# One core, a two-block transformer kernel: U and V expert gathers interleaved by head, V rows summed half on TensorE and half on VectorE

## The reference

```python
act = jax.nn.gelu(jnp.einsum('tkd,td->tk', expert_u[ib], xb))
return jnp.einsum('tk,tkd->td', act * gb, expert_v[ib])
```

## Time and profile before

| | us |
|---|---|
| three runs, median (lowest to highest) | 2695.06 (2687.06 to 2697.92) |
| the profiled execution | 2693.59 |
| its span | 2692.2 |
| busy VectorE / TensorE matmul / GpSimd / ScalarE | 1981.9 / 1236.9 / 1051.8 / 545.4 |
| first gather of the ring | at 613.11 |
| first transposes of h behind the last V row | at 1864.95 |

### The profile page before, as it was taken

The page is one execution under the profiler, slowest core; times in us unless marked ns, Lnnn a source line. Parts: engine busy times, 40 slices in busy tenths (PEclk is TensorE's granted clock), DMA queues, the critical chain, the costliest instruction groups (busy, mean ns, idle before and its releaser), DMA issues.

```text
span 2692.2 us, 14997 instructions
## 1 busy us (share of the span) xinstructions
PE 1236.9 (46%) x5498; PEld 1015.7 (38%) x5498; DVE 1981.9 (74%) x1974; ACT 545.4 (20%) x587; POOL 1051.8 (39%) x522
## 2 busy tenths in 40 slices
PE   7988886520000000000000000002999999999999
PEld 6876665420000000000000000002778878788887
DVE  3456557778999999999999999998454474654453
ACT  4244342110000000000000000001443343543342
POOL 0000001327877676768888888884000000000000
PEclk9999888765555555555555555556999999999999
DMA  5432346668999898989999999997445544445554
GB/s 212 155 131 104 110 160 238 243 221 360 422 422 420 347 377 355 375 357 414 422 422 422 422 422 422 422 422 286 160 156 190 200 150 157 171 173 192 195 184 147
DMA packets 104473, 750.93 MB, mean 279 GB/s; under 512 B 11856, under 2 KB 11856, under 8 KB 13264
## 3 DMA queue, kind: packets, MB, share of 16 engines
q0 software_dynamic: 73728, 536.90, 49.0%
q1 hardware_dynamic: 28512, 207.63, 21.7%
q10 hardware_dynamic: 2160, 5.45, 0.5%
HBM read 747.84 MB, written 2.10 MB: 279 GB/s over the span
## 4 chain that ended last, share of the span: by engine, by line
PE 35%; DVE 23%; POOL 23%; DMA 9%; issue 6%; ACT 3%; ACTq 0%; DVEq 0%; SPq 0%; POOLq 0%
POOL W L236 12%; PE ps L268 11%; POOL xT_rows L236 11%; PE ps L270 11%; PE ps L269 11%; DVE h L1365 10%; DMA W<-in_expert_u,idx 5%; DVE wlo L986 3%; DMA xT_rows<-in_expert_u,idx 3%; DVE W L1287 2%; ACT whi L639 1%; PE ps L295 1%; DVE xT_rows L1337 1%; DMA W<-in_expert_v,idx 1%; DVE tmp L1274 0%
## 5 line engine op out<-in xcount | busy, mean ns | idle before, releaser
L986 DVE TENSOR_TENSOR wlo<-raw,whi 128x2048 fp32r<-128x2048 f32 x195 | 446.4, 2290 | 372.3 <-ACT whi L639 372.0
L295 PE MATMUL ps<-ident,h 128*128 128x128 f32 x128 | 19.7, 310 | 1299.7 <-DVEq L1370 1289.7
L268 PE MATMUL ps<-whi,xT 128*128 128x512 f32 (+1 forms) x1432 | 576.4, 403 | 86.5 <-DVE wlo L986 84.7
L269 PE MATMUL ps<-wlo,xT 128*128 128x512 f32 (+1 forms) x1432 | 568.4, 397 | 0.0
L270 PE MATMUL ps<-whi,xT 128*128 128x512 f32 (+1 forms) x1432 | 567.7, 396 | 0.0
L236 POOL DMA_INDIRECT W<-in_expert_u,idx x144 | 280.7, 1949 | 585.1 <-DVE idx L1280 421.6
L295 PEld LDWEIGHTS ps<-ident,h 128*128 128x128 f32 x128 | 17.8, 162 | 1301.7 <-DVEq L1370 1290.2
L639 ACT ACTIVATE whi<-raw 128x2048 fp32r<-128x2048 f32 x195 | 372.8, 1914 | 492.6 <-PE ps L270 474.3
L268 PEld LDWEIGHTS ps<-whi,xT 128*128 128x128 f32 x1432 | 279.5, 195 | 155.2 <-DVE wlo L986 69.5
L236 POOL DMA_INDIRECT xT_rows<-in_expert_v,idx x128 | 272.0, 2125 | 107.1 <-DVE h L1365 61.9
L1365 DVE SCALAR_TENSOR_TENSOR h<-W,act,h 128x2048 f32<-128x2048 f32 x128 | 301.0, 2351 | 14.8 <-DMA W<-in_expert_v,idx 0.5
(11 more groups left out here) (230 smaller groups left out, 1073.0 us busy)
## 6 DMA issues: line engine op xcount, KB each, us to landing
raw<-in_weights SPq DMA_DIRECT2D x196, 1024.0 KB, 4.8
W<-in_expert_u,idx POOLq DMA_INDIRECT x144, 15.3
h<-in_x SPq DMA_DIRECT2D x2, 1024.0 KB, 6.9
xT_rows<-in_expert_v,idx POOLq DMA_INDIRECT x128, 14.1
W<-in_expert_v,idx POOLq DMA_INDIRECT x128, 14.1
out<-h ACTq DMA_DIRECT2D x8, 256.0 KB, 4.6
xT_rows<-in_expert_u,idx POOLq DMA_INDIRECT x112, 16.4
W<-in_pool_op ACTq DMA_DIRECT2D x1, 1024.0 KB, 15.4
```

Of the source, the lines that this page charges most:

```text
L268: pe.matmul(o, a[0], b[0], start=start, stop=False)
L269: pe.matmul(o, a[0], b[1], start=False, stop=False)
L295: m = pe.transpose(ps[:, bank, (2 * k + t) * 128:(2 * k + t + 1) * 128], src(t, 2 * g + k), ident[:, :])
L986: v.tensor_tensor(lo, raw[:, c % RAW, :], hi.bitcast(F32), ALU.subtract).then_inc(sem["lo_done"], 1)
```

## The change

The gathers follow a list, ROW_ORDER. A unit is the 16 rows of one head of one tile, 16 units for each table. U unit p + 2 and V unit p alternate row by row for p = 0 to 13, and V units 14 and 15 end the list alone. The 32 early U rows are units 0 and 1.

For a V row ScalarE scales the identity matrix by the weight column to a diagonal matrix (eight buffers), TensorE multiplies it with columns 0 to 1023 of the row (two f32 matmuls of 512 columns) and sums the rows of a tile in two PSUM banks. VectorE does the same `scalar_tensor_tensor` as before on columns 1024 to 2047 alone. A slot is free for the next gather when both are done. The two banks are added to h for tile 0 within unit 8 and for tile 1 at the end (`peer_in`).

The gates of tile 0 are made before the first row, those of tile 1 in unit 5; gelu and the product go by units of 16 columns. The splits of chunks 60 and 61 are made before the rows. `keys_later` and `experts_later` of two heads each stand in every one of the first four units. The core of the diff:

```diff
+UNITS = 16
+LAG = 2
+DIAGS = 8
+HALF = D // 2
+ROW_ORDER = [(kind, unit, j) for p in range(UNITS) for j in range(16) for kind, unit in (("u", p + LAG), ("v", p)) if unit < UNITS]
+ROW_AT = {what: n for n, what in enumerate(ROW_ORDER)}
...
+            for n, (kind, unit, j) in enumerate(ROW_ORDER):
+                if n >= GR:
+                    kind0, unit0, j0 = ROW_ORDER[n - GR]
+                    if kind0 == "u":
+                        g.wait_ge(sem["u_used"], 16 * (unit0 - LAG) + j0 + 1)
+                    else:
+                        g.wait_ge(sem["v_used"], 16 * unit0 + j0 + 1)
+                        g.wait_ge(sem["v_half"], 16 * unit0 + j0 + 1)
+                if kind == "u" and unit >= NH and j == 0:
+                    g.wait_ge(sem["idx1_ok"], unit - NH + 1)
+                t, c = unit // NH, 16 * (unit % NH) + j
+                gather(slots[n % GR], expert_u if kind == "u" else expert_v, t, c, row_in[n % GR])
...
-            pe.wait_ge(sem["v_done"], 2)
+            for unit in range(UNITS):
+                t = unit // NH
+                for j in range(16):
+                    n, i = ROW_AT["v", unit, j], 16 * unit + j
+                    pe.wait_ge(sem["diag_ok"], i + 1)
+                    pe.wait_ge(row_in[n % GR], 16 * (n // GR + 1))
+                    for b in range(2):
+                        m = pe.matmul(ps[:, (4 if t == 0 else 0) + b, :], diag[:, i % DIAGS, :], slots[n % GR][:, b * NC:(b + 1) * NC],
+                                      start=(unit % NH == 0 and j == 0), stop=(unit % NH == NH - 1 and j == 15))
+                    m.then_inc(sem["v_used"], 1)
+
+            pe.wait_ge(sem["peer_in"], 3)
+            pe.wait_ge(sem["v_half"], 16 * UNITS)
             entry(E_PLE, 0)
+            pe.wait_ge(sem["peer_in"], 4)
             entry(E_PLE, 1)
...
+            split(61)
+            gate_exps(0)
+            for unit in range(LAG):
+                gelu_unit(unit)
+            for unit in range(UNITS):
+                t = unit // NH
+                a.wait_ge(sem["w_ok"], unit + 1)
+                for j in range(16):
+                    i, c = 16 * unit + j, 16 * (unit % NH) + j
+                    if i >= DIAGS:
+                        a.wait_ge(sem["v_used"], i - DIAGS + 1)
+                    a.activation(diag[:, i % DIAGS, :], ident[:, :], ACT.Copy, scale=act[:, t, c:c + 1]).then_inc(sem["diag_ok"], 1)
+                    if j == 3 and LAG <= unit + 1 < UNITS:
+                        gelu_unit(unit + 1)
+                    if j == 3 and unit == 5:
+                        gate_exps(1)
...
+            split(60)
+            split(61)
+            gates_in(0)
+            gates_out(0)
+            for unit in range(LAG):
+                unit_weights(unit)
+            v.wait_ge(sem["query_out"], 8)
+            for p in range(UNITS):
+                for j in range(16):
+                    unit = p + LAG
+                    if unit < UNITS:
+                        t = unit // NH
+                        n, c = ROW_AT["u", unit, j], 16 * (unit % NH) + j
+                        v.wait_ge(row_in[n % GR], 16 * (n // GR + 1))
+                        v.tensor_tensor_reduce(slots[n % GR], slots[n % GR], xn[:, t, :], 1.0, 0.0, ALU.mult, ALU.add, act[:, t, c:c + 1]).then_inc(sem["u_used"], 1)
+                    t = p // NH
+                    n, i, c = ROW_AT["v", p, j], 16 * p + j, 16 * (p % NH) + j
+                    if j == 0:
+                        v.wait_ge(sem["w_ok"], p + 1)
                     v.wait_ge(row_in[n % GR], 16 * (n // GR + 1))
-                    v.scalar_tensor_tensor(h[:, t, :], slots[n % GR], act[:, t, c:c + 1], h[:, t, :], ALU.mult, ALU.add).then_inc(sem["rows_used"], 1)
+                    if i:
+                        v.wait_ge(sem["v_half"], i)
+                    v.scalar_tensor_tensor(h[:, t, HALF:], slots[n % GR][:, HALF:], act[:, t, c:c + 1], h[:, t, HALF:],
+                                           ALU.mult, ALU.add).then_inc(sem["v_half"], 1)
+                    if p < 4:
+                        if j in (2, 8):
+                            keys_later(2 * p + j // 8)
+                        if j in (5, 11):
+                            experts_later(2 * p + j // 11)
+                    if p == 5 and j == 0:
+                        gates_in(1)
+                    if p == 5 and j == 5:
+                        gates_out(1)
+                    if p == 8 and j == 4:
+                        v.wait_ge(sem["v_used"], 128)
+                        for b in range(2):
+                            peer_in(0, 4, b)
+                    if j == 8 and LAG <= p + 1 < UNITS:
+                        unit_weights(p + 1)
+            v.wait_ge(sem["v_used"], 16 * UNITS)
+            v.wait_ge(sem["v_half"], 16 * UNITS)
+            for b in range(2):
+                peer_in(1, 0, b)
```

More of the change, by code:

```diff
@@ L831, in scalar_program, with gate_exps, gelu_unit @@
                     m.then_inc(evac_of(b)[0], 1)
-            for t in range(NT):
+            def gate_exps(t):
                 a.wait_ge(sem["gate_in"], t + 1)
                 a.activation(gate[:, t, :], gate[:, t, :], ACT.Exp).then_inc(sem["gate_exp"], 1)
-                a.wait_ge(sem["u_done"], t + 1)
-                a.activation(act[:, t, :], act[:, t, :], ACT.Gelu_apprx_tanh).then_inc(sem["act_ok"], 1)
-            split(60)
+            def gelu_unit(unit):
+                t, c = unit // NH, 16 * (unit % NH)
+                if unit < LAG:
+                    a.wait_ge(sem["early_used"], 16 * (unit + 1))
+                else:
+                    a.wait_ge(sem["u_used"], 16 * (unit - LAG + 1))
+                a.activation(act[:, t, c:c + 16], act[:, t, c:c + 16], ACT.Gelu_apprx_tanh).then_inc(sem["act_ok"], 1)
+            split(60)
+            split(61)
[14 more added lines that the diff above has]
+                        gate_exps(1)
             entry(E_PLE, 0, C_GATE)
@@ L853, in scalar_program @@
                     c = C_GATE + 4 * n + qn
[L854 removed]
+                    if c + 1 > C_GATE + 1:
+                        split(c + 1)
                     if n == 0 and qn < 2:
@@ L1330, in experts_later, with gates_in @@
                              gate[:, 1, n * 16:(n + 1) * 16], nothing, sem["idx1_ok"])
[L1332 to L1343, removed]
+            def gates_in(t):
                 g3 = heads(gate[:, t, :], NH)
@@ L1369, in vector_program, with unit_weights, peer_in @@
-                v.wait_ge(sem["rows_used"], n)
-                v.nop().then_inc(sem["v_done"], 1)
-            split(60)
+            def unit_weights(unit):
+                t, cs = unit // NH, slice(16 * (unit % NH), 16 * (unit % NH) + 16)
+                v.wait_ge(sem["act_ok"], unit + 1)
+                v.tensor_tensor(act[:, t, cs], act[:, t, cs], gate[:, t, cs], ALU.mult).then_inc(sem["w_ok"], 1)
+            def peer_in(t, bank, b):
+                cs = slice(b * NC, (b + 1) * NC)
+                v.tensor_tensor(h[:, t, cs], ps[:, bank + b, :], h[:, t, cs], ALU.add).then_inc(sem["peer_in"], 1)
```

34 lines of the change are left out of this document (11 added, 23 removed).

## The result

The changed kernel takes 2651.38 us (median of four runs, 2649.50 to 2652.84) against 2694.31 for the kernel before: a ratio of 0.9844, 95% interval 0.9822 to 0.9866. Run once more beside the experiments it gave 2650.63, ratio 0.9832 (0.9806 to 0.9857). Forecast was 2643 with a range of 2636 to 2667. The profiled execution took 2652.54 us, 41 less than that of before, where 51.5 were forecast.

A forecast was written before the change was run, and what follows sets the result against it. Transfers bound at 2.485 us per 1 MB row, except in the first sum, where VectorE held DMA back 48 us. 2693.6 less 50.5 and 1 behind the phase gave 2642.1, or 2643 for a median; range 2636 to 2667.

The forecast's parts named there:

- What bounds the kernel: Transfers bound every stage except the first sum (V of tile 0), where VectorE holds DMA back by 48 us.
- VectorE, V row: VectorE's half of a V row takes 1.24 us, against 2.351 for the whole row before.
- TensorE, V row: TensorE's half of a V row: 4 records, 1.8 us at the high clock, 3.4 to 3.6 at the low.
- The blocks: Tile 1's key and expert choices, 72 us on VectorE in 64 pairs, cost 0; the ring bridges about 9.6 us of lag.
- Rival 1: Choice blocks are not bridged: 3 us for each expert block, 24 in all, giving 2667; chance 0.13.
- The pace: Transfers in the ring take 2.485 us per 1 MB row; 479 rows make 1190 us after the first landing.
- The start: Before the ring's first row, VectorE's splits and gates make it 2 us late, costing nothing; DMA starts as before.
- The end: Last row lands at 1811; the transposes of h follow at 1814.5 instead of 1864.95, 50.5 us earlier.
- rival 2: TensorE stays at the low clock in the last 32 rows: up to 32 us, 2675; chance 0.05.
- Rival 3: TensorE sets the pace at 5.5 us per V row, making the kernel slower: 2861; chance 0.05.
- Rival 4: Alternating two tables slows transfers to 2.57 us per row, so little changes: 2684; chance 0.05.
- The signs: Trace marks named beforehand: DMA share 1.01 if right; POOL waits released by TensorE for rivals; pace over 2.5 us if wrong.

The follow-up runs named there:

- e2: The changed kernel with the old order of gathers, keeping V rows halved between TensorE and VectorE: 2649.92 us, 0.9838 of the kernel before.
- e9: The kernel of e3 with V gathers of 1024 instead of 2048 columns, 512 KB each, of other rows: 2388.21 us, 0.8874 of the kernel before.
- e4: The changed kernel without the choice of tile 1's experts, indices and gates copied from tile 0: 2650.58 us, 0.9847 of the kernel before.
- e8: The changed kernel with all choice blocks of tile 1 packed into the first two units: 2667.49 us, 0.9914 of the kernel before.
- e5: The changed kernel with the ring's first gather no longer waiting for the last choice of tile 0: 2641.97 us, 0.9807 of the kernel before.
- e1: The changed kernel with its new gather order, but each V row summed whole on VectorE: 2679.97 us, 0.9952 of the kernel before.
- e3: The changed kernel without TensorE's half of the V sum, its diagonals and additions from PSUM: 2647.03 us, 0.9833 of the kernel before.
- e10: The changed kernel with each V row's two matmuls issued twice: 2679.96 us, 0.9966 of the kernel before.

## Why the prediction was right, and where it was off

*What bounds the kernel.* Right. That 48 us lay in the first sum alone and that the transfers bounded elsewhere is what e2 and e9 show; the phase fell by 42. (By the landings of the trace of before, the first sum took 47.7 us more than 128 steps of 2.485.)

*VectorE, V row*: forecast 1.24 us, measured 1.284. *TensorE, V row*: forecast 4 records, 1.8 us at the high level; the trace has 1024 records for 256 rows, 1.95 us from the first start to the last end of a row at the high level and 3.75 at the low one, where 3.4 to 3.6 was forecast; in the mixed part both occur. *ScalarE*: forecast 0.31 per diagonal, measured 0.40 in flow (the eight queued at the start go at 0.31). None of them is on the path, but for TensorE's last row.

*The blocks.* Taking 0 for them was right within 2 to 3 us (e4), and so was the reason, a bridge of about 9.6 us read from the earlier trace rows (e8, e5, and the 9 us in e1). Rival 1 fell.

*The pace.* This is the term that was mis-sized. The floor was taken as 479 rows of 2.485 us from one step of the earlier trace rows. From the first row to the last the changed kernel needed 1823.83 - 624.05 = 1199.8 us, 2.505 per row, where 1192.3 was forecast: 7.5 us too few. The step of 2.485 is right for most rows: it is the median of the 479 steps between landings. But twelve steps are longer than 2.8, by 9.5 us together, and the forecast allowed 2. In the trace of before this was to be seen, had I taken the mean of a stage instead of one step: 2.4995 per row in the U and in the V stage of tile 1. The 1.8 us that I took for an uneven start of the first stage are of the same kind: a slow first step, and a landing 0.95 us late at 784.6.

*The start.* The forecast said that nothing is lost there, and that DMA starts as before. The first two gathers of the changed kernel:

```profile
616.23 4.48 DVE L1037 TENSOR_TENSOR wlo<-raw,whi 128x2048 fp32r<-128x2048 f32 x2
617.03 2.29 POOL L244 DMA_INDIRECT xT_rows<-in_expert_u,idx  x1 [15.75 <-DVE idx L1331]
619.63 1.89 POOL L244 DMA_INDIRECT xT_rows<-in_expert_v,idx  x1 [0.31 <-issue]
...
624.05 2.29 DVE L1423 CUSTOM_DVE_ANT_0 xT_rows<-xT_rows,W 128x2048 f32<-128x2048 f32 x1 [0.70 <-DMA xT_rows<-in_expert_u,idx]
```

The gathers took 2.29 and 1.89 us where they took 0.94 before, when VectorE stood still; now it runs the two splits that the change has moved to this place. The first split ends at 618.51 and the first gather at 619.32, 0.81 later; the second split ends at 620.71 and the second gather at 621.52, 0.81 later again. That is no accident: of the 3997 gathers in the 13 traces that took over 1.05 us, 3984 end 0.81 us (within 0.04) after a VectorE instruction that was running when they began, or that began within 0.2 us of that. The other 13 are the first gather of each run. What VectorE reads matters. A TENSOR_REDUCE, with one input, does not hold a gather, and a TENSOR_TENSOR, with two, does, here in the changed kernel and in e5:

```profile
495.13 0.69 DVE L1327 TENSOR_REDUCE tmp<-tmp 128x32 f32<-128x512 f32 x1
495.20 0.93 POOL L244 DMA_INDIRECT W<-in_expert_u,idx  x1 [3.74 <-DVE act L1338]
```

```profile
608.30 0.76 DVE L1327 TENSOR_TENSOR tmp<-tmp 128x256 f32<-128x256 f32 x2
608.72 1.15 POOL L244 DMA_INDIRECT W<-in_expert_v,idx  x1 [0.31 <-issue]
```

The Trainium skill, "SBUF — State Buffer", section "Who interferes with whom", says that a VectorE instruction with two SBUF inputs contends with GpSimd's reads, through a port that both share; the split has two such inputs. The rows agree; that it is the port is the page's word, as the traces show only the times. The first row lands 7.0 us after its gather starts instead of 5.7, so it costs 1.4 us. In e5, where the first gathers stand beside short instructions and take 0.94 us, that is gone.

The forecast's reading of a gather in full flow was wrong by the same rows: what it shows beyond 0.94 us is not waiting for room but for VectorE. The gather at 1577.67 takes 1.44 us and ends 0.81 after the dot that began at 1576.02; the one at 1580.90 begins before the next dot and takes 0.94. In the ring this costs nothing that shows, as the DMA share stays at 1.01.

*The end.* From the last landing to the transposes 2.85 us, forecast 3.5. TensorE was at the high level from the first row of the tail on (1.95 us per row), so rival 2 did not come true. That was in part luck: of the last two V rows ahead of the tail the one at 1738.62 took 3.60 us, mostly at the low level, and the one at 1743.60 took 1.95. What a start at the low level costs was not run. Rival 3 fell too: TensorE could do twice its work in the mixed part (e10). Rival 4, slower transfers from two tables in turn, fell with the DMA lines: 422 GB/s, and e2 has the same phase.

*The signs.* Two of those named were poor. "POOL's waits released by TensorE" was to tell of rivals 2 and 3; the 311 us of such waits came, and e3 shows that they cost nothing. And a row pace over 2.5 us from 1000 to 1700 was to mean "wrong"; it was 2.499, with four late landings in it, so the sign only just stayed silent on the very term that was off.

*The sum.* 7.5 for the pace and 1.4 for the start, less 0.7 at the end, are 8.2 of the 8.4 us between the forecast 50.5 and the 42.1 measured for the phase (1260.6 - 1218.5). What else separates 51.5 from 41 is where the early stages ended: the last early dot came 3.9 us later in this profile. The 1 us expected behind the phase (2.8 in these two profiles) cannot be told from the scatter of 6 us between profiles of that part.

## What to carry to other kernels

Where two resources are nearly full, work out per stage which one ends last, and price a change by the stage in which its engine leads; shares over the whole span (74% against 46%) point at VectorE in all of them. A ring of buffers bridges a block of other work up to a fixed lag, here 9.4 to 11.2 us for eight slots of 1 MB, and beyond it every us is lost, so density decides and not the sum. Take a pace from a stage's first and last row, not from one step; and once the transfers bound, look at the waits ahead of the first one before moving arithmetic to yet another engine.

## What the runs showed that was not expected

- Landings that come about 0.95 us late stand behind packets of the DMA queue q14, of kind "instruction". In the changed kernel ten of the twelve long steps between landings have an 8 KB packet of it 1.5 to 3.3 us ahead. The late landing at 1586.86 has one at 1584.80; the DMA view of the window 1581 to 1587:

```profile
q0 software_dynamic: 347, 2.52, 101.2%
q14 instruction: 1, 0.01, 0.3%
```

  (Other packets of that queue, as the one at 1229.2, delay nothing.) The packets that do so come by how many instructions VectorE has run, not by gathers, bytes or time. From one to the next VectorE has 121 to 136 instruction records, its waits counted, while the gathers between them are 27 to 31 in the choice stretch and 60 to 64 behind it. With the choice blocks left out (e4) they are 58 and 62 there too. Twice the matmuls (e10) leave the distances as they are, and with half V gathers (e9) they are 64 and 63 gathers again, 120 us apart instead of 160, with the same 0.95 us. So this is most likely the loading of VectorE's program; how it delays a landing is not shown. Work on VectorE that the ring bridges is thus not quite free.
- TensorE's granted clock follows how closely its work is spaced. With four records per 4.97 us it goes up and down between its two levels from V row to V row, so that a row takes 1.95 us, 3.75, or something between, and the mean is 0.74 to 0.75; eight records in 3.67 us per 4.97 give 0.99 to 1.00 (e10); V rows 2.49 apart give 0.98 to 1.00 (the tail, and e2). The Trainium skill, "TensorE: Matmul & The Clock Gate", "What's actually happening", has the lower level as the default that activity releases; the rows agree, and at this spacing the level comes and goes.
